# Two attention streams at once: the reciprocal multiply of one stream moved from VectorE to GpSimd

## The chip, the core and the metric

The kernel runs on one core of one Trainium2 chip. The metric is the device time of one execution in microseconds (us); the time before is the median of three runs. The core's engines are TensorE (PE in the rows, with its weight loads as PEld), VectorE (DVE), ScalarE (ACT), GpSimd (POOL) and SyncE (SP), which here only issues DMAs. Each engine works through its own list of instructions in order, and the engines wait for each other with semaphores.

## The reference, cut to what matters

Two transformer blocks are computed one after the other, each two layers deep. The second block has two streams of 256 tokens and width 1024: the image, called A in the kernel, and the context, called B. The change touches only the softmax of the image's attention in the first layer of the second block:

```python
# image, heads 0 to 7: neighbourhood attention, with a bias table
logits = jnp.concatenate([s_nb.reshape(B, H, GRID_W, n_nb), s_ctx], axis=-1)
p = jax.nn.softmax(logits, axis=-1).astype(v.dtype)
...
# image, heads 8 to 15: windowed attention, with a sink column
p = jax.nn.softmax(jnp.concatenate([s_loc, s_ctx, sink_col], axis=-1), axis=-1).astype(v.dtype)
...
# context, in the first layer only: attention of the context to itself
p = jax.nn.softmax(s, axis=-1)[..., :C].astype(v.dtype)
```

A softmax here is: logits, their maximum per row, exponentials and their sum, the reciprocal of the sum, and the multiply of every probability by that reciprocal. The image attends to 256 image keys and 256 context keys, so a row of its probabilities has 512 numbers; a row of the context's has 256.

## The kernel before, in words

The kernel is written by hand: a table called ORDER lists visits, each one step of one stage of stream A or B, and every engine walks through the same table and emits its own part of each step. So the order of instructions on each engine is fixed when the kernel is built, and within an engine nothing overtakes anything else.

Matrix products with weights are done in three passes (a high and a low part of each operand, lines 991 to 993), with 512 KB units of weights streamed from HBM. The stage `att2` has no weights. It works through 16 groups g = 0 to 15; a group is a pair of heads by 128 query rows. For the image (A) in the first layer, while the context (B) attends too, a group k takes these steps on these engines:

- PE `scores` (L1157): logits of both heads against both key sets, into the PSUM slot of the group; each stream has two slots.
- DVE `maxima`: the bias table added (L2144, groups 0 to 7) or the window mask (L2139, groups 8 to 15), then the row maximum (L2147 or L2149), and for groups 8 to 15 a minimum with the sink (L2154).
- ACT `exp_half` (L1632), once per head: exponentials into PRA (two buffers), sums into SMA; for groups 8 to 15 also the sink's exponential (L1637).
- DVE `normalise`: for groups 8 to 15 the sink's term is added to the sum (L2163), then the reciprocal RIA (L2164), then the multiply of PRA by it, one instruction per head (L2166). The last one raises the semaphore `probs`.
- PE `probs_t` (L1166): eight transposes of PRA into the slot. It waits for `probs`.
- ACT `probs_t` (L1648): the transposed probabilities copied to PTSA.
- PE `weighted` (L1175): their product with V. ACT `y_part` (L1653): its high part H_hiA. DVE `result` (L2177): its low part H_loA, which frees the slot.

B does the same with 256 keys (PRB, PTSB, H_hiB, H_loB), some groups behind, in the same lists. On DVE a round of the joint loop reads: normalise A(k-1), maxima A(k), result B, normalise B, result A(k-1), maxima B, and then normalise A(k). In rounds 1 to 4 a part of A's rotary embedding (`q_rope`, four instructions of 128x1024) stands before the next normalise A. On ACT a round reads: copy PTSA, H_hiB, first exponential of A, H_hiA, second exponential of A, copy PTSB, the exponentials of B. On PE: probs_t A, weighted B, weighted A, scores B, probs_t B, scores A.

GpSimd has little to do: the first approximation of inverse square roots (`root`, L883), a fill and small DMAs of the bias table (L887, L895). Nothing of it falls into this loop except one `root` of stream B near its start.

The stage `att2` of the second layer runs with stream A alone (`st.solo`) and is not touched; nor is the attention of the first block.

Of the kernel before, what the change touches and what calls it, by code (L numbers as in the profile page):

```python
# [10 lines left out]
ALU = mybir.AluOpType  # L11
# [488 lines left out]
class Semaphores:  # L500


    def __init__(self, new):
        self.x_in = new("x_in")
        self.head_in = new("head_in")
        self.h0_hi = new("h0_hi")
        self.h0_ready = new("h0_ready")
        self.root_out = new("root_out")
        self.rooted = new("rooted")
        self.ctx_in = new("ctx_in")  # L510
        self.con_in = new("con_in")
        self.par_in = new("par_in")
        self.mask_in = new("mask_in")
        self.cond_in = new("cond_in")
        self.cond_ready = new("cond_ready")
        self.stored = new("stored")
        self.at_zero = new("at_zero")
        self.expo_ready = new("expo_ready")
        self.bt_low = new("bt_low")
        self.bt_in = new("bt_in")  # L520
        self.w_hi = new("w_hi")
        self.w_lo = new("w_lo")
        self.raw_in = [new(f"raw_in{i}") for i in range(RAW)]
        self.ada_in = [new(f"ada_in{i}") for i in range(ADA_RING)]
        self.mod_sums = new("mod_sums")
        self.gain_ready = new("gain_ready")
        self.dve_step = new("dve_step")
        self.glue = new("glue")
        self.sig = new("sig")
        self.tap = new("tap")  # L530
        self.gate_logits = new("gate_logits")
        self.gate_abs = new("gate_abs")
        self.gate_min = new("gate_min")
        self.gate_e = new("gate_e")
        self.gate_l = new("gate_l")
        self.gate_d = new("gate_d")
        self.gate_exps = new("gate_exps")
        self.gla_in = new("gla_in")
        self.kdT = new("kdT")
        self.attnT = new("attnT")  # L540
        self.attn_sb = new("attn_sb")
        self.d_state = new("d_state")
        self.state = new("state")
        self.gla_o = new("gla_o")
        self.r_act = new("r_act")
        self.r_gain = new("r_gain")
        self.mu = new("mu")
        self.centered = new("centered")
        self.ln_out = new("ln_out")
        self.ln_act = new("ln_act")  # L550
        self.mix_y = new("mix_y")
        self.mix_hi = new("mix_hi")
        self.og = new("og")


class StreamSemaphores:
# [51 lines left out]
def build_kernel(nc, xT, ctxT, wstream, adastream, par, const, imask, cond, outT):  # L608
    with ExitStack() as ctx:  # L609
# [179 lines left out]
        def groups2(s, st):  # L789

            window = con("causal", 512)[:, SEQ:2 * SEQ], con("band", 256)
            kv = [A, B] if s is A else [B]
            out = []
            for wa in range(2):
                for t in range(4):
                    for qt in range(2):
                        n = len(out)
                        kt, v0 = (4, 512) if wa else (t, P * t)
                        g = Group(st.grp + n, st.tok + st.proj.late + n, s.Q[:, 4 * wa + t, P * qt:P * qt + P],
                                  [o.K[:, kt, :] for o in kv],  # L800
                                  lambda h, kb, v0=v0: kv[kb // 2].V[:, kb % 2, v0 + 64 * h:v0 + 64 * h + 64],
                                  yi=16 * st.l + n, out=(4 * wa + t, slice(P * qt, P * qt + P)))
                        if wa:
                            g.sink = 2 * t
                            g.si = 8 * st.l + n - 8
                            if s is A:
                                g.window = window[qt]
                        elif s is A:
                            g.bias = (t, 2 - 2 * qt)
                        out.append(g)  # L810
            return out

        def buffers(s, st):
            return (PR1, PTS1) if st.kind == "mix1" else (s.PR, s.PTS)

# [62 lines left out]
        @block.gpsimd  # L878
        def _(pool):
            def root(s, rs, n):  # L880

                pool.wait_ge(s.sem.var, rs + 1)
                pool.tensor_tensor(s.R0[:, 0:n], s.V_[:, 0:n], EXPO[:, 0:n], ALU.pow).then_inc(s.sem.r0, 1)  # L883

            def bias_table(l):

                pool.memset(BT[:, :, :], BIG).then_inc(S.bt_low, 1)  # L887
                pool.wait_ge(S.bt_low, l + 1)
                o = _par[f"rpb{l}"]
                rows = par[0:64, o:o + 48].rearrange("(h r) e -> h r e", h=2)  # L890
                for c in range(64):
                    c0 = min(max(c - 8, 0), 48)
                    r = 15 + c0 - c
                    for h in range(2):
                        pool.dma_start(BT[64 * h + c:64 * h + c + 1, c0:c0 + 16, :], rows[h:h + 1, r:r + 16, :])\  # L895
                            .then_inc(S.bt_in, 16)

            def norm(s, st):
                yield
                root(s, st.rs, 2)  # L900
                yield
                yield
                yield

            def final(s, st):
                yield
                root(s, st.rs, 2)
                yield
                yield

            def mix1(s, st):
                for _ in range(33):
                    yield
                root(s, st.rs, 8)
                for _ in range(9):
                    yield
                root(s, st.rs + 1, 2)
                yield
                yield
                root(s, st.rs + 2, 8)  # L920
                for _ in range(6):
                    yield

            def ffn(s, st):
                for i in range(len(st.steps)):
                    if i == LATE_BIAS and st.blk == 1 and st.l == DEPTH - 1:
                        pool.wait_ge(s.sem.done, st.v)
                        bias_table(0)
                    if i == LATE_BIAS and s is A and st.blk == 2 and st.l == 0 and st.ffn == 1:
                        pool.wait_ge(s.sem.done, st.v)  # L930
                        bias_table(1)
                    yield

            def in2(s, st):
                parts = qk_parts(s, st)
                n = 0
                for u in st.steps:
                    if u is None:
                        if n % 2 == 0:
                            root(s, st.rs + n // 2, 4 * parts[n // 2][3])  # L940
                        n += 1
                    yield

            def att2(s, st):
                for k in range(len(st.steps)):
                    if st.proj.late and k == 1:
                        root(s, st.proj.rs + 3, 16)
                    yield

            def plain(s, st):  # L950
                for _ in st.steps:
                    yield

            table = dict(norm=norm, final=final, mix1=mix1, ffn=ffn, in2=in2, att2=att2, out2=plain, end=plain)
            pool.memset(EXPO[:, :], -0.5).then_inc(S.expo_ready, 1)
            pool.memset(AT[:, :, :], 0.0).then_inc(S.at_zero, 1)
            pool.wait_ge(S.expo_ready, 1)
            at_step = {}
            for v in ORDER:
                if v.i == 0:  # L960
                    at_step[v.stage] = table[v.stage.kind](streams[v.s], v.stage)
                next(at_step[v.stage])
# [917 lines left out]
        def _(dve):  # L1880
# [3 lines left out]
            def step(ins):  # L1884

                count.steps += 1
                ins.then_inc(S.dve_step, 1)
                dve.wait_ge(S.dve_step, count.steps)
# [268 lines left out]
            def normalise(s, st, g):  # L2157
                dve.wait_ge(s.sem.probs_exp, g.i + 1)
                b = g.i % 2
                pr = buffers(s, st)[0]  # L2160
                if g.sink is not None:
                    dve.wait_ge(s.sem.sink_exp, g.si + 1)
                    step(dve.tensor_tensor(s.SM[:, b, :], s.SM[:, b, :], s.ES[:, b, :], ALU.add))  # L2163
                step(dve.reciprocal(s.RI[:, b, :], s.SM[:, b, :]))  # L2164
                for h in range(2):
                    a = dve.tensor_scalar(pr[:, b, h, 0:g.nk], pr[:, b, h, 0:g.nk], s.RI[:, b, h:h + 1], None, ALU.mult)  # L2166
                a.then_inc(s.sem.probs, 1)
# [581 lines left out]
```

## Time and profile before

| | us |
|---|---|
| runs | 2515.51, 2522.3, 2524.03 |
| median | 2522.3 |
| the profiled execution, its own time | 2529.06 |
| its span, first to last instruction | 2527.3 |
| joint attention of the first layer, within the span | about 1213.6 to 1317.8 |

The span is what the rows below are cut from; start times in them are microseconds from the span's start. "Busy" counts an engine's instructions alone. A bracket at a row's end says how long the engine had been idle before it and what ended that idle time. Instructions overlap a little with the one ahead of them on their engine (the next starts while the last one drains), so start-to-start distances are more exact than sums of durations.

### The profile page before, as it was taken

Reading aid. Unit: us, or ns where it says so; the run is one execution under the profiler, and the core shown is the slowest. Engines: PE = TensorE matmul, PEld = TensorE weight load, DVE = VectorE, ACT = ScalarE, POOL = GpSimd, SP = SyncE. Lnnn points to the kernel's source line nnn. Section 1 sums busy time; section 2 is a strip of 40 time slices with the busy share of each in tenths; the row PEclk is TensorE's granted clock in tenths of the full one; section 3 lists DMA queues with packets and bytes.
Section 4 is the critical chain, followed back from the end, with each engine's and each line's share of the span. In section 5 each row is a group of like instructions: output and inputs, shape, how many; then the busy total and the mean of one; then the engine's idle time right before and its main releaser. Section 6 shows DMA issues by size and latency. Waiting matters only on the chain. (4 is left out here: it accounts for less than half of the span.)

```text
span 2527.3 us, 47682 instructions
## 1 busy us (share of the span) xinstructions
PE 2386.5 (94%) x20452; PEld 2316.5 (92%) x20452; DVE 1660.4 (66%) x2777; ACT 996.6 (39%) x1468; POOL 188.3 (7%) x300
## 2 busy tenths in 40 slices
PE   7889999899889999999789999999999999978999
PEld 7889998899889999999559999999999999966999
DVE  6778887689877777754684777776333335376554
ACT  6455554565532222232473322223322224145543
POOL 0000000190000000011000900000000000100000
PEclk9899998899989999999899999999999999999999
DMA  6246653357525555522002555552323323112554
GB/s 254 85 154 206 225 191 117 118 182 247 195 93 200 184 200 188 189 67 84 18 1 68 165 193 191 198 187 92 101 93 100 97 96 109 60 51 68 167 192 159
DMA packets 104306, 352.78 MB, mean 140 GB/s; under 512 B 18976, under 2 KB 19232, under 8 KB 103840
## 3 DMA queue, kind: packets, MB, share of 16 engines
q1 hardware_dynamic: 95904, 348.94, 40.6%
q8 instruction: 161, 2.64, 0.4%
q0 software_dynamic: 8192, 0.80, 0.3%
q14 instruction: 49, 0.40, 0.1%
HBM read 348.63 MB, written 1.05 MB: 138 GB/s over the span
## 5 line engine op out<-in xcount | busy, mean ns | idle before, releaser
L1519 ACT ACTIVATE W_hi<-W_raw 128x1024 fp32r<-128x1024 f32 x510 | 538.4, 1059 | 1075.1 <-PE slot L993 1012.6
L1895 DVE TENSOR_TENSOR W_lo<-W_raw,W_hi 128x1024 fp32r<-128x1024 f32 x510 | 622.0, 1222 | 456.2 <-ACT W_hi L1519 447.8
L991 PE MATMUL slot<-H_hiA,W_lo 128*128 128x256 f32 x2768 | 794.6, 287 | 25.4 <-DVE H_loA L2032 11.3
L992 PE MATMUL slot<-H_loA,W_hi 128*128 128x256 f32 x2768 | 783.2, 283 | 0.0
L993 PE MATMUL slot<-H_hiA,W_hi 128*128 128x256 f32 x2768 | 782.2, 283 | 0.0
L991 PEld LDWEIGHTS slot<-H_hiA,W_lo 128*128 128x128 f32 x2768 | 536.4, 194 | 38.5 <-issue 21.2
L993 PEld LDWEIGHTS slot<-H_hiA,W_hi 128*128 128x128 f32 x2768 | 536.0, 194 | 0.0
L992 PEld LDWEIGHTS slot<-H_loA,W_hi 128*128 128x128 f32 x2768 | 535.7, 194 | 0.1
L1907 DVE SCALAR_TENSOR_TENSOR PROD<-A_raw,SC 128x1024 bf16<-128x1024 f32 x288 | 341.2, 1222 | 152.6 <-DMA A_raw<-adastream 151.9
L991 PE MATMUL slot<-H_hiB,W_lo 128*128 128x256 f32 x1376 | 384.8, 280 | 3.7 <-DVE VB L2419 1.3
L993 PE MATMUL slot<-H_hiB,W_hi 128*128 128x256 f32 x1376 | 381.7, 277 | 0.0
L992 PE MATMUL slot<-H_loB,W_hi 128*128 128x256 f32 x1376 | 381.2, 277 | 0.0
L991 PE MATMUL slot<-HIDA,W_lo 128*128 128x256 f32 x1056 | 293.3, 278 | 1.5 <-DVE HIDA L2127 0.8
L992 PE MATMUL slot<-HIDA,W_hi 128*128 128x256 f32 x1056 | 293.0, 277 | 0.0
L993 PE MATMUL slot<-HIDA,W_hi 128*128 128x256 f32 x1056 | 293.0, 277 | 0.0
L991 PEld LDWEIGHTS slot<-H_hiB,W_lo 128*128 128x128 f32 x1376 | 259.5, 189 | 5.8 <-issue 2.2
L992 PEld LDWEIGHTS slot<-H_loB,W_hi 128*128 128x128 f32 x1376 | 259.3, 188 | 0.0
L993 PEld LDWEIGHTS slot<-H_hiB,W_hi 128*128 128x128 f32 x1376 | 259.1, 188 | 0.0
L991 PEld LDWEIGHTS slot<-HIDA,W_lo 128*128 128x128 f32 x1056 | 198.9, 188 | 2.1 <-issue 1.2
L993 PEld LDWEIGHTS slot<-HIDA,W_hi 128*128 128x128 f32 x1056 | 198.8, 188 | 0.0
L992 PEld LDWEIGHTS slot<-HIDA,W_hi 128*128 128x128 f32 x1056 | 198.3, 188 | 0.0
L883 POOL TENSOR_TENSOR R0A<-V_A,EXPO 128x2 f32<-128x2 f32 (+3 forms) x25 | 38.7, 1549 | 1999.1 <-DVE V_A L1933 1999.1
(277 smaller groups left out, 3050.5 us busy)
## 6 DMA issues: line engine op xcount, KB each, us to landing
W_raw<-wstream SPq DMA_DIRECT2D x510, 512.0 KB, 3.3
A_raw<-adastream SPq DMA_DIRECT2D x144, 512.0 KB, 4.6
BT<-par POOLq DMA_DIRECT2D x256, 3.0 KB, 2.7
XA<-xT SPq DMA_DIRECT2D x2, 512.0 KB, 4.6
SC<-cond SPq DMA_DIRECT2D x1, 1024.0 KB, 14.4
XB<-ctxT SPq DMA_DIRECT2D x1, 1024.0 KB, 16.4
CON<-const SPq DMA_DIRECT2D x1, 960.5 KB, 9.5
PAR<-par SPq DMA_DIRECT2D x1, 680.0 KB, 10.7
```

The costliest lines, as they stand in the source:

```text
L883: pool.tensor_tensor(s.R0[:, 0:n], s.V_[:, 0:n], EXPO[:, 0:n], ALU.pow).then_inc(s.sem.r0, 1)
L991: pe.matmul(out, wl, xh, start=start, stop=False, skip_group_check=True)
L992: pe.matmul(out, wh, xl, start=False, stop=False, skip_group_check=True)
L993: return pe.matmul(out, wh, xh, start=False, stop=stop, skip_group_check=True)
L1519: act.activation(W_hi[:, g % HIGH, :], W_raw[:, g % RAW, :], ACT.Copy).then_inc(S.w_hi, 1)
L1895: dve.tensor_tensor(W_lo[:, g % RAW, :], W_raw[:, g % RAW, :], W_hi[:, g % HIGH, :].bitcast(F32), ALU.subtract).then_inc(S.w_lo, 1)
L1907: a = dve.scalar_tensor_tensor(PROD[:, b, :], A_raw[:, slot, :], 1.0, SC[:, b, :], ALU.mult, ALU.mult, accum_out=MOD[:, t // MODS, t % MOD ...
```

## The change

For the image's groups in the joint `att2` (stream A, second block, first layer), DVE computes the reciprocal and raises a new semaphore `inverse` instead of doing the two multiplies. GpSimd waits for it, does the two multiplies of 128x512, and raises `probs`. The GpSimd part stands in A's step 3(k+1) of the stage, the same step in which DVE has the normalise of group k. Everything else keeps its place.

```diff
+        def scaled_by_pool(s, st):
+            return s is A and st.kind == "att2" and not st.solo
...
             def att2(s, st):
+                gs = groups2(s, st)
                 for k in range(len(st.steps)):
                     if st.proj.late and k == 1:
                         root(s, st.proj.rs + 3, 16)
+                    if scaled_by_pool(s, st) and k % 3 == 0 and 0 < k <= 3 * len(gs):
+                        g = gs[k // 3 - 1]
+                        b = g.i % 2
+                        pool.wait_ge(S.inverse, k // 3)
+                        for h in range(2):
+                            a = pool.tensor_scalar(s.PR[:, b, h, 0:g.nk], s.PR[:, b, h, 0:g.nk], s.RI[:, b, h:h + 1],
+                                                   None, ALU.mult)
+                        a.then_inc(s.sem.probs, 1)
                     yield
...
                     step(dve.tensor_tensor(s.SM[:, b, :], s.SM[:, b, :], s.ES[:, b, :], ALU.add))
+                if scaled_by_pool(s, st):
+                    dve.reciprocal(s.RI[:, b, :], s.SM[:, b, :]).then_inc(S.inverse, 1)
+                    return
                 step(dve.reciprocal(s.RI[:, b, :], s.SM[:, b, :]))
```

On VectorE, one round of the joint loop with the rotary part behind it (groups with a bias) reads before, with the semaphores each instruction waits for in brackets (`scoresA` is raised by PE, `probs_exp` and `y_hi` by ACT, `evac` by DVE itself):

```order
L2164 RECIPROCAL RIA<-SMA 128x2 [waits probs_expA]
L2166 TENSOR_SCALAR PRA<-PRA,RIA 128x512 [waits dve_step]
L2166 TENSOR_SCALAR PRA<-PRA,RIA 128x512
L2144 TENSOR_TENSOR slot<-slot,BT 128x2x256 [waits scoresA]
L2147 TENSOR_REDUCE NMA<-slot 128x2 [waits dve_step]
L2177 TENSOR_TENSOR H_loB<-slot,H_hiB 128x128 [waits evacB,y_hiB]
L2164 RECIPROCAL RIB<-SMB 128x2 [waits probs_expB]
L2166 TENSOR_SCALAR PRB<-PRB,RIB 128x256 [waits dve_step]
L2166 TENSOR_SCALAR PRB<-PRB,RIB 128x256
L2177 TENSOR_TENSOR H_loA<-slot,H_hiA 128x128 [waits evacA,y_hiA]
L2147 TENSOR_REDUCE NMB<-slot 128x2 [waits scoresB]
```

The same round on VectorE in the changed kernel (its line numbers are up to 16 higher):

```order
L2178 RECIPROCAL RIA<-SMA 128x2 [waits probs_expA]
L2157 TENSOR_TENSOR slot<-slot,BT 128x2x256 [waits scoresA]
L2160 TENSOR_REDUCE NMA<-slot 128x2 [waits dve_step]
L2193 TENSOR_TENSOR H_loB<-slot,H_hiB 128x128 [waits evacB,y_hiB]
L2180 RECIPROCAL RIB<-SMB 128x2 [waits probs_expB]
L2182 TENSOR_SCALAR PRB<-PRB,RIB 128x256 [waits dve_step]
L2182 TENSOR_SCALAR PRB<-PRB,RIB 128x256
L2193 TENSOR_TENSOR H_loA<-slot,H_hiA 128x128 [waits evacA,y_hiA]
L2160 TENSOR_REDUCE NMB<-slot 128x2 [waits scoresB]
```

The two multiplies of PRA are gone, and nothing else has moved against anything else.

On GpSimd, around the start of the second block's first attention, the list before holds only roots (`R0A`, `R0B`; 128x16 are those of queries and keys) and then the bias table of the next layer:

```order
L883 TENSOR_TENSOR R0B<-V_B,EXPO 128x4 [waits varB]
L883 TENSOR_TENSOR R0A<-V_A,EXPO 128x16 [waits varA]
L883 TENSOR_TENSOR R0B<-V_B,EXPO 128x16 [waits varB]
L883 TENSOR_TENSOR R0A<-V_A,EXPO 128x2 [waits varA]
L883 TENSOR_TENSOR R0B<-V_B,EXPO 128x2 [waits varB]
L887 MEMSET BT 128x3072 [waits doneA]
```

In the changed kernel the same place of GpSimd's list begins:

```order
L887 TENSOR_TENSOR R0B<-V_B,EXPO 128x4 [waits varB]
L887 TENSOR_TENSOR R0A<-V_A,EXPO 128x16 [waits varA]
L958 TENSOR_SCALAR PRA<-PRA,RIA 128x512 [waits inverse]
L958 TENSOR_SCALAR PRA<-PRA,RIA 128x512
L887 TENSOR_TENSOR R0B<-V_B,EXPO 128x16 [waits varB]
L958 TENSOR_SCALAR PRA<-PRA,RIA 128x512 [waits inverse]
L958 TENSOR_SCALAR PRA<-PRA,RIA 128x512
```

Sixteen such pairs stand there in all; one pair is ahead of B's root of 16 columns and fifteen behind it, all ahead of the next layer's bias table. The lists of PE and ACT are unchanged.

## Rows read from the trace of the kernel before

**Rows 1.** The page, busy time, share of the span and instructions of two engines.

```profile
PE 2386.5 (94%) x20452; PEld 2316.5 (92%) x20452; DVE 1660.4 (66%) x2777; ACT 996.6 (39%) x1468; POOL 188.3 (7%) x300
```

**Rows 2.** Busy time by stretch: PE, PEld, DVE, ACT, POOL, granted clock, DMA share, GB/s.

```profile
1246.00:1317.80 71.80, 58.71 (x562) 40.88 (x560) 63.21 (x159) 56.66 (x171) 0.00 (x0) 1.00 0.01 1
...
1230.00:1240.00 10.00, 5.90 (x49) 4.27 (x49) 7.24 (x13) 5.46 (x13) 0.00 (x0) 0.83 0.00 1
```

**Rows 3.** Timeline of DVE, one round with a bias: start, duration, what, idle before.

```profile
1262.65 0.88 DVE L2166 TENSOR_SCALAR PRA<-PRA,RIA 128x512 f32<-128x512 f32 x2
1263.50 1.05 DVE L2144 TENSOR_TENSOR slot<-slot,BT 128x512 f32<-128x512 f32 x1
...
1267.24 0.29 DVE L2177 TENSOR_TENSOR H_loA<-slot,H_hiA 128x128 fp32r<-128x128 f32 x1 [0.29 <-ACT H_hiA L1653]
1267.57 0.69 DVE L2147 TENSOR_REDUCE NMB<-slot 128x2 f32<-128x512 f32 x1
1268.18 0.15 DVE L2164 RECIPROCAL RIA<-SMA 128x2 f32<-128x2 f32 x1
1268.37 0.88 DVE L2166 TENSOR_SCALAR PRA<-PRA,RIA 128x512 f32<-128x512 f32 x2
```

**Rows 4.** Timeline of PE in the same round.

```profile
1263.59 1.09 PE L1166 MATMUL slot<-CON,PRA 128*128 128x128 f32 x8
...
1265.79 0.66 PE L1175 MATMUL slot<-PTSA,VA 128*64 128x128 f32 x8 [0.53 <-ACT PTSA L1648]
...
1268.57 0.60 PE L1157 MATMUL slot<-KB,QA 64*128 64x256 f32 x4
1269.30 1.09 PE L1166 MATMUL slot<-CON,PRA 128*128 128x128 f32 x8
```

**Rows 5.** Timeline of ACT in the same round.

```profile
1264.72 1.02 ACT L1648 ACTIVATE PTSA<-slot 128x1024 f32<-128x1024 f32 x1 [0.78 <-PE slot L1166]
...
1266.93 0.28 ACT L1653 ACTIVATE H_hiA<-slot 128x128 fp32r<-128x128 f32 x1 [0.31 <-PE slot L1175]
```

**Rows 6.** Timeline of DVE, one round with window mask and sink.

```profile
1310.79 0.88 DVE L2166 TENSOR_SCALAR PRA<-PRA,RIA 128x512 f32<-128x512 f32 x2
1311.59 0.69 DVE L2139 TENSOR_TENSOR slot<-slot,CON 128x512 f32<-128x512 f32 x1
...
1314.08 0.29 DVE L2177 TENSOR_TENSOR H_loB<-slot,H_hiB 128x128 fp32r<-128x128 f32 x1 [0.35 <-ACT H_hiB L1653]
...
1316.91 0.88 DVE L2166 TENSOR_SCALAR PRA<-PRA,RIA 128x512 f32<-128x512 f32 x2
```

**Rows 7.** Tile PRA, window 1200 to 1320: min/median/max ns, first and last start.

```profile
L2166 DVE TENSOR_SCALAR PRA<-PRA,RIA x32: 478/484/488, 1213.8 to 1317.3; 128x512 f32<-128x512 f32 x32
```

**Rows 8.** Timeline of PE: probs_t A of the first and the last group.

```profile
1214.71 1.09 PE L1166 MATMUL slot<-CON,PRA 128*128 128x128 f32 x8 [2.61 <-DVE PRA L2166]
...
1317.85 1.09 PE L1166 MATMUL slot<-CON,PRA 128*128 128x128 f32 x8 [1.60 <-DVE PRA L2166]
```

**Rows 9.** Groups of POOL by line and shape: busy us, mean ns, idle before.

```profile
L883 POOL TENSOR_TENSOR R0A<-V_A,EXPO 128x2 f32<-128x2 f32 x13 | 9.1, 701 | 1693.7 <-DVE V_A L1933 1693.7
...
L887 POOL MEMSET BT<- 128x3072 f32 x2 | 5.3, 2668 | 0.0
...
L956 POOL MEMSET AT<- 128x1024 f32 x1 | 1.0, 952 | 0.0
```

**Rows 10.** Timelines: DVE and then POOL at a root of stream A.

```profile
1197.60 0.17 DVE L1933 TENSOR_SCALAR V_A<-slot 128x16 f32<-128x16 f32 x1 [2.41 <-PE slot L1056]
...
1197.85 2.90 POOL L883 TENSOR_TENSOR R0A<-V_A,EXPO 128x16 f32<-128x16 f32 x1 [1.80 <-DVE V_A L1933]
```

**Rows 11.** Timelines of PE and ACT in an early round, at the lower granted clock.

```profile
1236.14 1.63 PE L1166 MATMUL slot<-CON,PRA 128*128 128x128 f32 x8 [1.72 <-DVE PRA L2166]
...
1238.89 1.12 PE L1175 MATMUL slot<-PTSA,VA 128*64 128x128 f32 x8 [1.11 <-ACT PTSA L1648]
...
1240.91 0.28 ACT L1653 ACTIVATE H_hiA<-slot 128x128 fp32r<-128x128 f32 x1 [1.40 <-PE slot L1175]
```

More of the change, by code:

```diff
@@ L553, in __init__ @@
         self.og = new("og")
+        self.inverse = new("inverse")
 class StreamSemaphores:
```

## The prediction

> **What bounds the kernel now.** I began with the page's busy times [rows 1]: TensorE is busy 94% of the span and GpSimd 7%. That says that TensorE sets most of the time and that GpSimd has room, but not what sets the joint attention, so I cut that stretch out. From 1246.0 to 1317.8 TensorE is busy 58.71 of 71.80 us, VectorE 63.21, ScalarE 56.66, and DMA does nothing [rows 2]. No engine is full. VectorE comes nearest, at 88%, which looks like the bound that the change relieves. But it is idle 8.6 us in these 12 rounds, 0.7 us a round, and an engine that bounds a loop has no idle time. So I looked for the loop of waits.
>
> In a round with a bias it can be followed from the end of one multiply of PRA to the end of the next, by start times:
> - multiply ends 1263.53 (1262.65 plus 0.88) [rows 3]; TensorE's transposes of PRA start 1263.59, 0.06 later [rows 4];
> - ScalarE's copy to PTSA starts 1264.72, 1.13 later [rows 5];
> - weighted A starts on TensorE 1265.79, 1.07 later, after 0.53 us in which TensorE waited for PTSA [rows 4];
> - H_hiA on ScalarE 1266.93, 1.14 later, having waited for TensorE [rows 5];
> - result A on VectorE 1267.24, 0.31 later, having waited 0.29 us for H_hiA; then maxima B 1267.57, 0.33 later; reciprocal A 1268.18, 0.61; multiply 1268.37, 0.19; its end 1269.25, 0.88 [rows 3].
>
> 0.06 + 1.13 + 1.07 + 1.14 + 0.31 + 0.33 + 0.61 + 0.19 + 0.88 = 5.72 us, which is the whole round (1269.25 - 1263.53). It closes because VectorE's list has result A(k-1) ahead of reciprocal A(k). Every multiply of PRA is a link of it. In rounds with a sink the round is 1316.91 - 1310.79 = 6.12 us; there VectorE waits 0.35 us at result B for H_hiB [rows 6], which stands behind the copy to PTSA in ScalarE's list, so the multiply of A is again a link, by way of TensorE's transposes and that copy.
>
> **The change part by part.** It takes 32 multiplies of 0.484 us from VectorE [rows 7], 0.88 us for a pair since two overlap by 0.08 [rows 3]. What that frees on VectorE lets the bias or mask add and the maximum of A start 0.88 us earlier. I cost this gain at nothing: the exponentials that want the maximum stand behind the copy to PTSA in ScalarE's list, and the copy wants the transposes, which want the multiply. VectorE only reaches its waits at result B and result A earlier and waits there longer. The cover would be gone only if the multiply ended sooner than now.
>
> It puts into the chain, in place of 0.88 us: a hand-over to GpSimd and a pair of GpSimd multiplies. The hand-over: from the reciprocal's start to the multiply's on VectorE is 0.19 us now [rows 3]. A reciprocal of 0.15 plus the hand-over from VectorE to GpSimd, 0.08 us (V_A ends at 1197.77, the root starts at 1197.85 [rows 10]), is 0.23: 0.04 more. The hand-over to TensorE stays at the 0.06 that it takes from VectorE.
>
> The pair has no row, since GpSimd does no such multiply in the kernel before. Bounds from its nearest rows: two fills give a slope of (2668 - 952) / 2048 = 0.838 ns a column and 0.094 us fixed [rows 9]. A multiply must write as much as a fill: 512 columns take 0.43 us, so a pair that overlaps its fixed part takes at least 2 x 0.43 + 0.09 = 0.95 us. For the other end: roots of 2 and of 16 columns take 0.70 and 2.90 us [rows 9, 10], which leaves a fixed part of 0.70 - 2 x 0.157 = 0.39 us for an instruction that reads operands. If every instruction pays that and reading comes on top of writing, one is 0.39 + 2 x 0.43 = 1.25 and a pair 2.50 us. I take 1.50 for the pair: one pass of 0.43 plus a fixed part between 0.09 and 0.39 gives 1.04 to 1.64, and some cost for reading puts it near the upper one of these.
>
> On the speed of such an operation, the Trainium skill's "GPSIMD Engine Reference", section 3.1, gives 1.03 cycles an element where the ports bound it and about 1.8 for a tight loop, at 1.2 GHz; as an estimate from that page that is 0.44 or 0.77 us for 512 elements, 0.88 or 1.54 us for a pair. The fills here agree with the first figure (0.838 ns is 1.006 cycles of 1.2 GHz), and nothing in this trace decides between the two for a multiply. With the second, the sum below would be 11 us; with the first, it would be next to nothing before the fixed cost of the two instructions.
>
> So a round becomes longer by 0.04 + 1.50 - 0.88 = 0.66 us, with 0.11 and 1.66 as its ends. How many rounds: VectorE has 32 multiplies, 16 pairs [rows 7]. The first is on the path, since TensorE waited 2.61 us for it and has B's sums of squares next in its list; so is the last, for which it waited 1.60 us [rows 8]; those between close the loop above, with the rotary parts in rounds 1 to 4 as an extra link that stays. Behind the stage TensorE is the bound again, and no wait of the joint loop is for a weight or a DMA, so I see nothing that gives the delay back. 16 x 0.66 = 10.6 us; the ends are 16 x 0.11 = 1.8 and 16 x 1.66 = 26.6 us.
>
> The added wait on GpSimd has B's root of 16 columns queued behind it, once. The first pair would end around 1213.58 + 0.23 + 1.50 = 1215.3, and that root waits for its operand until after 1218 in the trace before, so nothing there is late.
>
> The profiled execution would go from 2529.06 to 2539.7 us. It lies 6.8 us above the median of the runs, so for the runs I say 2522.3 + 10.6 = 2532.9, which is 0.42% slower. A measurement of this kernel tells about 0.3%, 7.6 us, from no change.
>
> **The rivals.**
> 1. *The GpSimd multiply is quick, and nothing measurable happens.* The same section's neighbour, 4.1 of "GPSIMD Engine Reference" in the Trainium skill, says that one-input elementwise work runs roughly at line rate there; no row here shows a multiply. As a mechanism of this kernel: the delay stays under 7.6 us if the pair takes less than 7.6 / 16 + 0.84 = 1.31 us. At one pass each and half the fixed part of a root, 2 x (0.43 + 0.20) = 1.26, hence 16 x 0.42 = 6.7 us, or 2529.0. At a fill's cost it is 1.8 us, 2524. The fills speak for it, the roots' fixed part against. This is the rival on the other side, not slower, and it decides at 1.31 us. Chance 0.27.
> 2. *VectorE is the bound and its relief pays.* If the pair cost nothing at all, a bias round could fall only to TensorE's own loop: scores A has its last four products issued at 1268.57 and lasting 0.60 [rows 4], so they end at 1269.17, and the transposes, now at 1269.30, would gain some 0.13 us; rounds with a sink at most VectorE's wait of 0.35 and that again, some 0.5; early rounds 0.84. 4 x 0.84 + 4 x 0.13 + 8 x 0.5 = 7.9 us faster at the very most, 2514. It needs a pair below 0.84 us, under the fill's own slope. Chance of faster by over 0.3%: 0.03.
> 3. *The two engines get in each other's way.* GpSimd's pair now runs while VectorE does the bias or mask add. If the adds went first and GpSimd had to wait until they end, each round pays most of 1.05 us (eight rounds [rows 3]) or 0.69 us (eight rounds [rows 6]): less 0.08 of hand-over, 8 x 0.97 + 8 x 0.61 = 12.6 us on top, 2545.5. Against it: these adds read one operand from PSUM. The Trainium skill's "SBUF — State Buffer", section Who interferes with whom, says that GpSimd and VectorE share one port pair under an exclusive lock, but that a VectorE instruction with one SBUF input outside its two-port modes does not take it. VectorE's multiply of PRB cannot meet the pair, since it stands behind a result B that waits for the pair's outcome. Chance 0.08.
> 4. *The longer gaps cost TensorE its clock.* From 1246 on it was granted full speed (2.4 GHz) [rows 2]. In the early rounds, after waits of 1.1 to 2.6 us [rows 8, 11], the granted clock of a stretch of 10 us was 0.83, a mix of both levels [rows 2]; the transposes then took 1.63 instead of 1.09 us and weighted A, from its start to H_hiA, 2.02 instead of 1.14 [rows 4, 5, 11]. If the rounds from 1251 on, 11 of them, fell to 1.2 GHz, each would pay 0.54 + 0.88 = 1.42 us, 15.6 in all: 2548.5. It takes effect once a wait of some 0.5 us before the transposes grows enough; I can't place that point. Chance 0.12.
>
> **How the numbers follow.** The main case, a pair of 1.31 to 2.0 us (2530 to 2541), gets 0.50. Slower in all is 0.50 + 0.08 + 0.12 = 0.70; within 0.3% is 0.27; faster 0.03. The forecast is 2533. The range: downwards it takes in most of rival 1, to 2524 (the fill's cost); upwards the middle of rivals 3 and 4 and all but the end of the pair's bound, to 2548. Some 0.08 is left out below and 0.10 above.
>
> **What the profile after would show.** A GpSimd pair of about 1.5 us, starting some 0.23 us after each reciprocal of A; bias rounds of 6.4 us and sink rounds of 6.8 us instead of 5.72 and 6.12; TensorE's wait before the transposes of PRA now put down to GpSimd and longer by about 0.6 us; VectorE waiting about 1.5 us more a round at result B or result A, with its busy time 14 us less; the rest of the span unchanged. I would be wrong if the rounds stay at 5.72 us with a pair above 0.95 us (then VectorE's order was the loop, not the multiply's latency), if the pair is outside 0.95 to 2.5 us, if an add in PSUM stretches or the pair starts only when it ends, or if the granted clock from 1250 on is below 1.00.

## The result and the profile after

The changed kernel takes 2572.57 us (median of three, 2572.31 to 2574.37) against 2522.3: a ratio of 1.020, with a 95% interval of 1.017 to 1.023. It is slower, as forecast, but by 50 us, nearly five times the 10.6 us of the forecast. The profiled execution took 2572.57 us itself, with a span of 2570.7.

The page after, its line of busy times; it answers to [rows 1]:

```profile
PE 2400.9 (93%) x20452; PEld 2325.6 (90%) x20452; DVE 1647.1 (64%) x2745; ACT 996.4 (39%) x1468; POOL 237.6 (9%) x332
```

VectorE lost 13 us of busy time and GpSimd gained 49. A pair of multiplies that took VectorE 0.88 us takes GpSimd 3.10 us, 3.5 times as long. Tile PRA after, in window 1200 to 1370 (min/median/max ns), answering to [rows 7]:

```profile
L958 POOL TENSOR_SCALAR PRA<-PRA,RIA x32: 1558/1562/1570, 1206.5 to 1358.2; 128x512 f32<-128x512 f32 x32
```

The timeline of GpSimd after, four rounds:

```profile
1267.55 3.10 POOL L958 TENSOR_SCALAR PRA<-PRA,RIA 128x512 f32<-128x512 f32 x2 [5.96 <-DVE RIA L2178]
1275.55 3.10 POOL L958 TENSOR_SCALAR PRA<-PRA,RIA 128x512 f32<-128x512 f32 x2 [4.89 <-DVE RIA L2178]
1284.61 3.10 POOL L958 TENSOR_SCALAR PRA<-PRA,RIA 128x512 f32<-128x512 f32 x2 [5.97 <-DVE RIA L2178]
1292.80 3.10 POOL L958 TENSOR_SCALAR PRA<-PRA,RIA 128x512 f32<-128x512 f32 x2 [5.09 <-DVE RIA L2178]
```

The first interval is a bias round of 8.00 us, and the chain of [rows 3 to 5] gives that within 0.02 with the measured pair: 5.72 + 0.04 + 3.10 - 0.88 = 7.98. But the next is 9.06 us long. The timeline of TensorE in that longer round shows why; it answers to [rows 4]:

```profile
1278.70 1.09 PE L1179 MATMUL slot<-CON,PRA 128*128 128x128 f32 x8 [2.41 <-POOL PRA L958]
1279.72 1.07 PE L1188 MATMUL slot<-PTSB,VB 128*64 128x128 f32 x8
1280.91 1.12 PE L1188 MATMUL slot<-PTSA,VA 128*64 128x128 f32 x8
```

Weighted A's first half took 0.66 us in [rows 4] and takes 1.12 here: the lower of the two clock levels, after a wait of 2.41 us for GpSimd. The timeline of VectorE in the round ahead of it, answering to [rows 3]:

```profile
1267.30 0.15 DVE L2178 RECIPROCAL RIA<-SMA 128x2 f32<-128x2 f32 x1
1268.34 1.02 DVE L2157 TENSOR_TENSOR slot<-slot,BT 128x512 f32<-128x512 f32 x1 [0.88 <-PE slot L1170]
1269.39 1.23 DVE L2160 TENSOR_REDUCE NMA<-slot 128x2 f32<-128x1024 f32 x1
1273.06 0.29 DVE L2193 TENSOR_TENSOR H_loB<-slot,H_hiB 128x128 fp32r<-128x128 f32 x1 [2.44 <-ACT H_hiB L1666]
```

VectorE spends the time that it was relieved of, and more, in waiting: 0.88 us for the scores of A and 2.44 us for H_hiB. GpSimd starts 0.25 us after the reciprocal (1267.55 against 1267.30); 0.23 was worked out.

The stage from A's first reciprocal to its last, before and after, by stretch (PE, PEld, DVE, ACT, POOL busy, granted clock):

```profile
1213.58:1316.71 103.13, 81.07 (x724) 58.73 (x724) 82.18 (x195) 66.24 (x193) 2.90 (x1) 0.92 0.01 2
```

```profile
1206.29:1356.41 150.12, 98.53 (x724) 72.04 (x724) 70.11 (x165) 66.50 (x193) 49.46 (x31) 0.80 0.00 1
```

It grew by 46.99 us. The latency added to a round is 0.04 + 3.10 - 0.88 = 2.26 us; 15 rounds of it are 33.9, and 13.1 us are left. The same stage, cut behind its fifth round, first before and then after:

```profile
1213.58:1256.74 43.16, 30.54 (x246) 23.52 (x248) 29.41 (x58) 17.83 (x47) 2.90 (x1) 0.80 0.01 2
1256.74:1316.71 59.97, 50.52 (x480) 35.21 (x480) 52.76 (x139) 48.41 (x147) 0.00 (x0) 1.00 0.01 1
```

```profile
1206.29:1267.30 61.01, 39.18 (x246) 30.00 (x248) 25.50 (x47) 17.80 (x47) 18.45 (x11) 0.66 0.00 1
1267.30:1356.41 89.11, 59.34 (x480) 42.04 (x480) 44.61 (x119) 48.70 (x147) 31.01 (x20) 0.89 0.00 1
```

In both parts the granted clock fell. The first five rounds grew by 17.85 us, 11.3 of it latency, the last ten by 29.14, 22.6 of it latency: what is left is 6.5 us in each part.

From the last reciprocal to the first matmul of the next stage it was 1326.51 - 1316.71 = 9.80 us and is 1370.62 - 1356.41 = 14.21: 4.4 more, of which the latency of the sixteenth group is 2.26; its transposes took 1.97 us, at the lower clock, instead of 1.09. Together 51.4, against 50.3 between the medians. The two profiled spans differ by 43.4 only, since the stage began 7.3 us earlier in the execution after (1206.29 against 1213.58), ahead of any changed instruction; that start lay between 1196.7 and 1216.9 in the traces below, most of them of kernels that are alike up to there. So I compare this stage's length, and times by their ratio. On the chips of the experiments, executions of the kernel before spread from 2509 to 2538 us.

### The profile page after: what moved, and what is told of

The parts are those of the page before. It is cut to its first block and busy times, and to the rows that moved or that the text cites. A ratio compares the mean times of both kernels' runs of the same rounds, so it can differ in the third digit from the quotient of the medians.

```text
span 2570.7 us, 47682 instructions
## 1 busy us (share of the span) xinstructions
PE 2400.9 (93%) x20452; PEld 2325.6 (90%) x20452; DVE 1647.1 (64%) x2745; ACT 996.4 (39%) x1468; POOL 237.6 (9%) x332
## 3 DMA queue, kind: packets, MB, share of 16 engines
HBM read 348.63 MB, written 1.05 MB: 136 GB/s over the span
```

## The experiments

A ratio below sets the executions of a version against 22 to 31 executions of the kernel before, timed beside them; their medians were 2520.8 to 2523.6 us. It comes with its 95% interval, and need not be the quotient of two medians to the last digit.

**Latency at the same place, made by VectorE.** Five more VectorE instructions into a scratch tile, between the reciprocal and the multiplies.

```diff
                 step(dve.reciprocal(s.RI[:, b, :], s.SM[:, b, :]))
+                if s is A and st.kind == "att2" and not st.solo:
+                    for w in (512, 512, 512, 512, 8):
+                        step(dve.tensor_scalar(SCR[:, 0:w], pr[:, b, 0, 0:w], s.RI[:, b, 0:1], None, ALU.mult))
```

> The kernel before, with five extra VectorE multiplies into a scratch tile (four of 512 columns, one of 8) between the reciprocal and the two multiplies of each of the 16 joint groups of A: about 4 x 0.52 + 0.19 = 2.3 us more latency at the very place where GpSimd's pair adds 0.04 + 3.10 - 0.88 = 2.26 us, with GpSimd left out. Latency theory: bias rounds at full clock 5.72 + 2.3 = 8.0 us, sink rounds 8.4 us, and the whole time about that of the changed kernel, 2568 to 2577 us. Interference theory (GpSimd's accesses slow VectorE or ScalarE): the time stays well below the changed kernel's, under 2560 us.

Measured: 2570.18 us, ratio 1.019 (1.015 to 1.023), the change's own loss. The stage, from first to last reciprocal:

```profile
1214.07:1365.27 151.20, 98.35 (x724) 71.87 (x724) 114.64 (x269) 66.60 (x193) 2.90 (x1) 0.80 0.00 1
```

151.20 us against the changed kernel's 150.12, with GpSimd out of it, and the same granted clock of 0.80. The delay is 2.36 us a round here instead of 2.26. So what costs is latency between reciprocal and transposes, whoever causes it.

**The gaps filled.** The changed kernel, with dummy transposes where TensorE waits.

```diff
+                p, pr = group_ps(st, g), buffers(s, st)[0]
+                if s is A and st.kind == "att2" and not st.solo:
+                    pe.wait_ge(s.sem.probs_exp, g.i + 1)
+                    for n in range(14):
+                        pe.transpose(p[:, n // 4 % 2, P * (n % 4):P * (n % 4) + P], ident, ident)
                 pe.wait_ge(s.sem.probs, g.i + 1)
-                p, pr = group_ps(st, g), buffers(s, st)[0]
```

> The changed kernel, with 14 dummy transposes of the identity on TensorE ahead of each group's transposes of A's probabilities, issued once the exponentials are there, into the place that the true ones then overwrite; they fill some 1.9 of the 2.4 us in which TensorE waits for GpSimd. Clock theory: 2.26 us x 16 = 36 us of the loss is latency and about 13 us is the lower granted clock that follows from the longer gaps; with the gaps filled the clock is 1.00 from about 1260 on, every full round is 8.0 or 8.4 us, and the time is 2557 to 2563 us. Rival (the clock is not tied to the gaps): granted clock as in the changed kernel, time the same or up to 10 us longer.

Measured: 2558.1 us, ratio 1.016 (1.012 to 1.020). The stage, and the timeline of TensorE in one of its rounds:

```profile
1216.94:1354.92 137.98, 106.41 (x928) 82.04 (x927) 70.12 (x164) 65.83 (x193) 49.49 (x31) 0.93 0.01 2
```

```profile
1281.07 1.75 PE L1179 MATMUL slot<-CON 128*128 128x128 f32 x14
1283.56 1.09 PE L1183 MATMUL slot<-CON,PRA 128*128 128x128 f32 x8 [0.74 <-POOL PRA L958]
```

The wait before the transposes of PRA is 0.74 us instead of 2.41, the clock 0.93 instead of 0.80, and the stage 12.1 us shorter, with more work in it. From 1260 on the clock is 1.00. What the stage still has over the kernel before is 34.85 us, near the 33.9 of latency. So the second part of the loss is TensorE's clock, and it hangs on TensorE's idle time. This rests on the stage in the traces: by the whole time the interval of this version still overlaps the changed kernel's 1.017 to 1.023.

**Relief alone.** VectorE's joint multiplies left out, nothing in their place: this kernel leaves the image's probabilities unnormalised, and the reciprocal itself releases TensorE.

```diff
+        def scaled_by_pool(s, st):
+            return s is A and st.kind == "att2" and not st.solo
...
+                if scaled_by_pool(s, st):
+                    dve.reciprocal(s.RI[:, b, :], s.SM[:, b, :]).then_inc(s.sem.probs, 1)
+                    return
                 step(dve.reciprocal(s.RI[:, b, :], s.SM[:, b, :]))
```

> The kernel before with the 32 joint multiplies of A left out altogether (the image's probabilities of the second block's first layer stay unnormalised); the reciprocal itself releases TensorE. It is what relief of VectorE could give at the very best. Latency theory: early rounds lose up to 0.88 us, bias rounds 0.1 to 0.3 us since TensorE's own loop is next, sink rounds 0.5 to 0.9 us: 6 to 12 us faster than before, with VectorE's waits growing. If VectorE's busy time were the bound: 16 x 0.88 = 14 us faster and VectorE's waits unchanged.

Measured: 2512.04 us, ratio 0.9965 (0.994 to 0.999). Its stage, and VectorE's timeline over one sink round:

```profile
1206.94:1298.43 91.49, 77.71 (x724) 56.47 (x724) 69.64 (x165) 67.17 (x193) 2.90 (x1) 0.94 0.01 2
```

```profile
1281.88 0.17 DVE L2170 RECIPROCAL RIA<-SMA 128x2 f32<-128x2 f32 x1
1282.53 0.70 DVE L2144 TENSOR_TENSOR slot<-slot,CON 128x512 f32<-128x512 f32 x1 [0.48 <-PE slot L1162]
...
1287.40 0.17 DVE L2170 RECIPROCAL RIA<-SMA 128x2 f32<-128x2 f32 x1
```

The stage is 11.6 us shorter. Sink rounds are 5.52 us, and VectorE now waits for the scores. TensorE's only wait in such a round is 0.53 us for the copy of its own transposes, so TensorE's loop is next. That is the most that relief of VectorE from these multiplies could bring here.

**GpSimd's prices, away from the stage.** A row of instructions on a scratch tile during the first feed-forward; each waits for the one ahead of it.

```diff
+                        for w in (64, 128, 256, 512):
+                            for _ in range(4):
+                                one(pool.tensor_scalar(SCR[:, 0:w], SCR[:, 0:w], ptr, None, ALU.mult))
...
+                        for _ in range(32):
+                            one(pool.tensor_scalar(SCR[:, :], SCR[:, :], ptr, None, ALU.mult))
```

> The kernel before, with a row of GpSimd instructions on a scratch tile during the first feed-forward of the first block, where nobody waits for GpSimd: multiplies by a pointer scalar at 64, 128, 256 and 512 columns, by an immediate at 128 and 512, copies, two-input multiplies, then 32 more multiplies of 512 columns. If the 1.56 us are the instruction's own, a multiply of 512 columns takes 1.56 us here too, with a slope of some 2.5 to 2.9 ns a column; if they come from the joint stage (contention with VectorE), it takes 0.5 to 0.9 us here. A pointer scalar may be what costs: then the immediate form is near 0.5 us. VectorE's W_lo subtractions read two SBUF tiles: if they and GpSimd exclude each other, some of them take up to 1.5 us longer than 1.22, and the time may grow by a few us; else 2522.

Measured: 2523.07 us, ratio 1.001 (0.999 to 1.003). Tile SCR (min/median/max ns):

```profile
L954 POOL TENSOR_SCALAR SCR<-SCR,SCB x32: 1565/2255/3379, 213.4 to 285.9; 128x512 f32<-128x512 f32 x32
...
L949 POOL COPY SCB<-SCR x8: 293/402/1169, 198.1 to 202.4; 128x128 f32<-128x128 f32 x4, 128x256 f32<-128x256 f32 x4
```

At its quickest, a multiply of 512 columns takes 1.565 us here too: it is the instruction's own price. (By an immediate the quickest was 1.49.) But many took longer, up to 3.38 us. Groups of VectorE from 205 to 240, in the kernel before and in this one:

```profile
L1895 DVE TENSOR_TENSOR W_lo<-W_raw,W_hi 128x1024 fp32r<-128x1024 f32 x12 | 14.7, 1224 | 6.5 <-ACT W_hi L1519 6.0 <-DVEq L1946 0.5
L2098 DVE SCALAR_TENSOR_TENSOR U<-slot,PAR,U 128x255 f32<-128x255 f32 x12 | 4.9, 475 | 0.0
```

```profile
L1924 DVE TENSOR_TENSOR W_lo<-W_raw,W_hi 128x1024 fp32r<-128x1024 f32 x12 | 18.6, 1573 | 0.5 <-DVEq L1975 0.5
...
L2127 DVE SCALAR_TENSOR_TENSOR U<-slot,PAR,U 128x255 f32<-128x255 f32 x12 | 4.9, 467 | 0.0
```

VectorE's subtraction, with two inputs in SBUF, takes 1.57 us instead of 1.22, while U<-slot,PAR,U, with a tensor in PSUM, keeps its 0.47. The two engines do get in each other's way, but not in an instruction that, like the bias and mask adds beside the pair, has one input in PSUM. It cost nothing measurable here; that fits with VectorE's 6.5 us of idle time in this stretch before, but wasn't tested.

**Half the columns.** GpSimd multiplies the first 256 columns of each head; the other 256 this kernel leaves unscaled.

```diff
-                            a = pool.tensor_scalar(s.PR[:, b, h, 0:g.nk], s.PR[:, b, h, 0:g.nk], s.RI[:, b, h:h + 1],
+                            a = pool.tensor_scalar(s.PR[:, b, h, 0:SEQ], s.PR[:, b, h, 0:SEQ], s.RI[:, b, h:h + 1],
```

> The changed kernel with GpSimd multiplying only the first 256 of the 512 columns of each head (the other 256 stay unscaled). If the cost is per column, 2.5 ns, an instruction takes about 0.93 us and the pair 1.86: full rounds at 2.4 GHz of 5.72 + 0.04 + 1.86 - 0.88 = 6.74 us with a bias and 7.14 with a sink, 16 us of latency in all, and 2537 to 2546 us, by how much of the clock is lost with gaps of some 1.2 us. If the cost is mostly fixed, it stays near 2570.

Measured: 2547.78 us, ratio 1.009 (1.006 to 1.012). Tile PRA, and the timeline of GpSimd:

```profile
L958 POOL TENSOR_SCALAR PRA<-PRA,RIA x32: 917/922/930, 1206.1 to 1328.4; 128x256 f32<-128x256 f32 x32
```

```profile
1264.31 1.82 POOL L958 TENSOR_SCALAR PRA<-PRA,RIA 128x256 f32<-128x256 f32 x2 [4.89 <-DVE RIA L2178]
1271.02 1.82 POOL L958 TENSOR_SCALAR PRA<-PRA,RIA 128x256 f32<-128x256 f32 x2 [4.89 <-DVE RIA L2178]
```

(1562 - 922) / 256 = 2.5 ns a column, and 0.28 us fixed. For 64 columns this gives 0.44 us; the quickest multiply of 64 columns among GpSimd's prices above took 0.446. The round is 6.71 us, by the chain 5.72 + 0.04 + 1.82 - 0.88 = 6.70. The stage took 1327.28 - 1205.86 = 121.42 us, 18.3 more than before, 14.7 of it latency: at this length of gap the clock costs 3.6 us. The median lies just above the range that I gave.

**One head each.**

```diff
-                        for h in range(2):
+                        for h in range(1, 2):
...
+                    dve.wait_ge(S.inverse, g.i - st.grp + 1)
+                    dve.tensor_scalar(pr[:, b, 0, 0:g.nk], pr[:, b, 0, 0:g.nk], s.RI[:, b, 0:1], None, ALU.mult)\
+                       .then_inc(s.sem.probs, 1)
...
+                    if h and scaled_by_pool(s, st):
+                        pe.wait_ge(S.second, g.i - st.grp + 1)
```

> The changed kernel with the work divided: VectorE multiplies head 0, GpSimd head 1, each with a semaphore of its own, and TensorE transposes head 0 while head 1 is still being multiplied. From the reciprocal's start to the copy to PTSA it took 0.19 + 0.88 + 0.06 + 1.13 = 2.26 us before; now 0.25 + 1.56 + 0.06 + 0.6 = 2.47 us if the two multiplies run side by side: 0.2 us more a round, 3 us in all, 2524. If they exclude each other, since VectorE's runs two columns a cycle, the second starts only when the first ends: GpSimd after VectorE gives 0.45 more a round (bias rounds about 6.4 us, in all 10 us, 2531); VectorE after GpSimd shows as a VectorE multiply of some 1.8 us.

Measured: 2533.5 us, ratio 1.004 (1.002 to 1.007). Timelines of VectorE and of GpSimd in one round:

```profile
1255.72 0.49 DVE L2183 TENSOR_SCALAR PRA<-PRA,RIA 128x512 f32<-128x512 f32 x1
```

```profile
1255.78 1.86 POOL L959 TENSOR_SCALAR PRA<-PRA,RIA 128x512 f32<-128x512 f32 x1 [4.46 <-DVE RIA L2181]
1262.29 1.86 POOL L959 TENSOR_SCALAR PRA<-PRA,RIA 128x512 f32<-128x512 f32 x1 [4.65 <-DVE RIA L2181]
```

GpSimd's multiply starts 0.06 us behind VectorE's and takes 1.86 us instead of 1.56: of the 0.43 us in which the two overlap it loses 0.30 to VectorE's, which keeps its 0.49. Bias rounds are 6.3 us, near the 6.4 that I had expected for two multiplies that exclude each other.

**GpSimd beside the chain.** The kernel before, with a scratch pair of multiplies on GpSimd once VectorE's multiply has ended.

```diff
+                        pool.wait_ge(s.sem.probs, g.i + 1)
+                        for h in range(2):
+                            pool.tensor_scalar(SCR[:, :], SCR[:, :], SCB[:, 0:1], None, ALU.mult).then_inc(S.tried, 1)
+                            pool.wait_ge(S.tried, 2 * (k // 3) + h + 1)
```

> The kernel before, with the same pair of GpSimd multiplies of 128x512 for each joint group of A, but on a scratch tile, started when VectorE's multiply of the group has ended, and nobody waits for it. Latency theory: GpSimd is busy 3.1 us a round and the round stays 5.72 or 6.12 us, the stage 103 us and the time 2521 to 2526; only where the pair reaches into VectorE's multiply of PRB may some tenths of a us be lost. Interference theory (GpSimd's work slows the joint stage by itself): the stage grows by 15 us or more.

Measured: 2526.08 us, ratio 1.002 (1.000 to 1.003); the stage 1318.58 - 1214.07 = 104.51 us. VectorE's timeline over a sink round:

```profile
1287.97 0.17 DVE L2178 RECIPROCAL RIA<-SMA 128x2 f32<-128x2 f32 x1
...
1290.96 0.62 DVE L2168 TENSOR_TENSOR NMA<-NMA,NS 128x2 f32<-128x2 f32 x1
...
1292.09 0.76 DVE L2180 TENSOR_SCALAR PRB<-PRB,RIB 128x256 f32<-128x256 f32 x2
...
1294.09 0.17 DVE L2178 RECIPROCAL RIA<-SMA 128x2 f32<-128x2 f32 x1
```

Beside GpSimd's pair the multiply of PRB takes 0.76 instead of 0.62 us, and the minimum with the sink, which reads two tiles in SBUF, 0.62 instead of 0.16, and the round still is 6.12 us. About the same 3.1 to 3.2 us of GpSimd a round cost 1.4 us in the stage where nobody waits for them, and 47 where TensorE does.

**The chain shortened.** The kernel before, with probs released head by head, in every attention.

```diff
                 for h in range(2):
-                    a = dve.tensor_scalar(pr[:, b, h, 0:g.nk], pr[:, b, h, 0:g.nk], s.RI[:, b, h:h + 1], None, ALU.mult)
-                a.then_inc(s.sem.probs, 1)
+                    dve.tensor_scalar(pr[:, b, h, 0:g.nk], pr[:, b, h, 0:g.nk], s.RI[:, b, h:h + 1], None, ALU.mult)\
+                       .then_inc(s.sem.probs, 1)
...
-                pe.wait_ge(s.sem.probs, g.i + 1)
                 p, pr = group_ps(st, g), buffers(s, st)[0]
                 for h in range(2):
+                    pe.wait_ge(s.sem.probs, 2 * g.i + h + 1)
```

> The kernel before with VectorE's multiply releasing TensorE head by head in every attention, so that the transposes of head 0 run beside the multiply of head 1; no work is added or taken away. Latency theory: the chain loses about 0.5 us a round; TensorE's own loop holds bias rounds at 5.5 us or above (0.2 gained), sink rounds go from 6.12 to about 5.6 us, early ones gain 0.45: 5 to 8 us faster, the joint stage about 96 instead of 103 us. If VectorE's busy time were the bound, nothing: 2521.

Measured: 2514.28 us, ratio 0.9964 (0.9945 to 0.9984): faster by 0.36%, as much as leaving the multiplies out (0.35%) within the intervals. Its stage, and VectorE's timeline:

```profile
1213.57:1310.17 96.60, 79.70 (x724) 57.76 (x724) 81.53 (x194) 67.20 (x193) 2.90 (x1) 0.93 0.01 2
```

```profile
1298.73 0.17 DVE L2164 RECIPROCAL RIA<-SMA 128x2 f32<-128x2 f32 x1
...
1301.82 0.29 DVE L2177 TENSOR_TENSOR H_loB<-slot,H_hiB 128x128 fp32r<-128x128 f32 x1
...
1304.45 0.17 DVE L2164 RECIPROCAL RIA<-SMA 128x2 f32<-128x2 f32 x1
```

Sink rounds went from 6.12 to 5.72 us, and the wait of 0.35 us at H_loB is gone. Only now does VectorE go through a sink round without any wait, so that its busy time bounds it. The stage is 6.5 us shorter; the edit also touches the other attentions, so the 0.36% need not all come from here.

**The early gaps filled, in the kernel before.** Eight dummy transposes, as above, ahead of the first five groups.

```diff
+                if s is A and st.kind == "att2" and not st.solo and g.i - st.grp < 5:
+                    pe.wait_ge(s.sem.probs_exp, g.i + 1)
+                    for n in range(8):
+                        pe.transpose(p[:, n // 4 % 2, P * (n % 4):P * (n % 4) + P], ident, ident)
```

> The kernel before with 8 dummy transposes of the identity ahead of the transposes of A's probabilities in the first five groups, where TensorE waits 0.8 to 2.6 us for them. Clock theory: the granted clock between 1215 and 1246, which is 0.69 to 0.83 before, rises, and the stage becomes 2 to 4 us shorter. Rival: those stretches are slow for what went ahead of them (the idle time up to 1215), the filling does nothing, or costs up to 3 us where 8 transposes at the lower clock take 2 us.

Measured: 2517.81 us, ratio 0.998 (0.996 to 1.000), so by the time it is open whether anything was gained. The stage:

```profile
1207.29:1306.97 99.68, 81.06 (x756) 58.80 (x756) 82.17 (x195) 66.25 (x193) 2.90 (x1) 0.97 0.01 2
```

In this trace it is 3.45 us shorter, at a granted clock of 0.97 instead of 0.92.

**Both.** The diffs of the last two experiments together.

> The kernel before with both of the edits that shortened the stage one at a time: VectorE releases TensorE head by head, and 8 dummy transposes of the identity stand ahead of the transposes of A's probabilities in the first five groups. From the first reciprocal of A to the last the stage took 103.13 us before, 96.60 with the first edit, 99.68 with the second. If the gains are of different kinds (latency of the chain, clock of TensorE) they add up: 93 to 94 us, and 9 to 12 us faster in all. If the dummies now delay the earlier first transposes, 95 to 97 us and 6 to 9 us faster.

Measured: 2511.14 us, ratio 0.9966 (0.995 to 0.998). VectorE's timeline, first and last reciprocal of A:

```profile
1204.95 0.16 DVE L2168 RECIPROCAL RIA<-SMA 128x2 f32<-128x2 f32 x1
...
1299.51 0.17 DVE L2168 RECIPROCAL RIA<-SMA 128x2 f32<-128x2 f32 x1
```

94.56 us, 8.6 less than before: in the stage the gains add up, to somewhat less than their sum of 10.0. The whole time can't tell this version from the one with the per-head release alone. Both are faster than the kernel before and the changed one.

## Why the prediction was wrong

**The bound: right.** The chain from multiply to multiply is what sets a round. With the measured pair it gives full-speed rounds to 0.02 us in three kernels (8.00, 6.71, and 8.08 with VectorE's delay of 2.36), and relief of VectorE in the changed kernel went into its waits. The direction was right with it.

**The gain costed at nothing: right.** VectorE gave up 13 us of busy time and the stage got none of it.

**The term that failed: the size of GpSimd's pair.** I took 1.50 us, between 0.95 and 2.50; it is 3.10. The step at fault is that I priced the multiply's columns at the slope of a fill, 0.838 ns, once for 1.50 us and twice (reading on top of writing) for the upper bound. The multiply takes 2.5 ns a column, three times as much. The fixed part, 0.28 us, was within what I had. The rows gave a warning that I passed over: the roots, the only instructions there that compute, cost 0.157 us a column, and I used their fixed part alone. The multiply lies between the two. So no useful bound from the nearest rows existed above, and I gave one all the same: a fill says how fast a column can be written, not how slowly one can be computed. With 2.26 us a round the sum is 36.2 us instead of 10.6.

The Trainium skill's "GPSIMD Engine Reference", section 3.1, gives 1.03 and 1.8 cycles an element, at 1.2 GHz, and its section 4.1 roughly line rate for one input. At that clock 2.5 ns are 3.0 cycles, so the multiply is slower than all of these; the measurement decides.

**The second step: the clock stood among the rivals, at 0.12, and the sum had nothing for it.** It came on top of the latency. The granted clock of the stage fell from 0.92 to 0.80, and filling the gaps gave back 12.1 us in the stage. My price for it, 15.6 us, was near the 13.1 that latency leaves open, but partly by luck: I had it from 11 late rounds, all at the lower level, and nothing from the early ones, which brought half of it. I had written that it takes effect once the wait of 0.5 us grows enough; with a wait of 2.41 us six of the last ten rounds took 9.1 to 9.5 us instead of 8.0 or 8.4, and with the pair 1.28 us shorter (half width) only the first rounds were slow. With the pair at 3.10 us the two go together, so its chance should have hung on the pair's size.

**The other rivals.** A quick GpSimd multiply: no. VectorE as the bound: no, with 13 us less to do it waits longer, and the time grows. Interference: right that it exists, and right that the loss doesn't come from it, since a delay of VectorE's own at the same place costs the same. The bias add took 1.02 us beside GpSimd's multiply (1.05 before), the pair 3.10 to 3.12 in every round. This is what the Trainium skill's "SBUF — State Buffer", section Who interferes with whom, says of an instruction with one SBUF input. The minimum with the sink, which GpSimd's scratch pair stretched to 0.62 us, kept its 0.16 in the changed kernel. One collision did occur in the changed kernel, where the multiply of PRB came early: VectorE's timeline of round 2, with GpSimd's pair running from 1235.56 to 1238.66:

```profile
1235.39 1.00 DVE L2157 TENSOR_TENSOR slot<-slot,BT 128x512 f32<-128x512 f32 x1
...
1237.75 1.06 DVE L2182 TENSOR_SCALAR PRB<-PRB,RIB 128x256 f32<-128x256 f32 x2
```

The two multiplies in it one by one (min/median/max ns):

```profile
L2182 DVE TENSOR_SCALAR PRB<-PRB,RIB x2: 353/572/791, 1237.8 to 1238.0; 128x256 f32<-128x256 f32 x2
```

1.06 instead of 0.62 us, with a wait for H_hiA of 5.2 us behind it that hides it. The first of the two, inside GpSimd's second multiply, took its usual 0.35 us and only the other was held up, so GpSimd doesn't shut VectorE out here for the whole of an instruction. My sentence that this multiply "cannot meet the pair" was wrong for the first group of B, which has no result B ahead of it.

**The ceiling of a gain: too low.** I gave 7.9 us for a free pair; without the multiply the stage is 11.6 us shorter, and the shortfall is in the early rounds. Their stretch without the multiply, to set beside the 43.16 us and 0.80 before:

```profile
1206.94:1242.89 35.95, 27.89 (x246) 21.28 (x248) 25.09 (x48) 17.93 (x47) 2.90 (x1) 0.86 0.01 2
```

Five rounds gained 7.2 us, at a higher granted clock, where I had 4 x 0.84 = 3.4; how much of it is the clock is not shown. The ten rounds behind gained 4.4 us, against my 4.5: TensorE's loop is 5.52 us there, below the 5.59 that I used, and sink rounds fall to it as well.

What stays open: why the clock falls in some rounds and not in others with the same wait (8.00 and then 9.06 us), why some overlaps of the two engines cost time and others none, and whether GpSimd's 2.5 ns a column holds for other operations; a copy of 256 columns took 0.40 us, less than half of a multiply.

## What to carry to other kernels

Before work is moved off the busiest engine, close the loop of waits around it: an engine that is 88% busy but waits each round is a link of a chain, and the replacement is priced by its latency in the chain, not by the time it frees. A price that no row shows has no upper bound from rows of simpler operations; run the one instruction alone first, it costs one kernel. Shortening the same link, by releasing the next engine after the first half (in every attention), gave 0.36% where moving it lost 2%.

## What the runs showed of the hardware

A GpSimd multiply by a per-partition scalar takes 0.28 us plus 2.5 ns a column in f32 (0.922 us at 256 columns, 1.562 at 512), against VectorE's 0.350 and 0.484. Run against a VectorE instruction that reads two SBUF tensors, or a VectorE multiply within SBUF, the two hold each other up: GpSimd's multiply took 1.86 instead of 1.56 us in the split kernel and up to 3.38 beside the weight subtractions, which took 1.57 on average instead of 1.22. A VectorE instruction with one input in PSUM kept its time. TensorE's granted clock was kept up by dummy transposes in its gaps: 0.93 instead of 0.80 over the stage, worth 12 us.
